# A transformer block on one core: the last expert pair's down projection as one half and two quarters of the columns, the last quarter scattered in fp32, and each token tile finished and stored by itself

## What is computed

```python
def _expert_choice_ffn(h, w_router, w_e_gate, w_e_up, w_e_down):
    cap = EC_CAPACITY * s // N_EXPERTS          # 64 tokens for each of 16 experts
    aff = softmax(h @ w_router)
    vals, idx = lax.top_k(swapaxes(aff, 1, 2), cap)
    xg = h[idx]
    a, u = xg @ w_e_gate, xg @ w_e_up           # (64, 2048) @ (2048, 1024), each expert
    y = (silu(a) * u) @ w_e_down                # (64, 1024) @ (1024, 2048)
    return zeros(s, d).at[idx].add(y * vals)

x = x + gt2 * _expert_choice_ffn(h2, ...)
return _rmsnorm(x, g_final)                     # x * rsqrt(mean(x * x) + eps) * g_final
```

## Time and profile before

| | |
|---|---|
| median of 3 runs | 2383.43 us (2383.26 to 2383.95) |
| span of the profiled execution | 2385.8 us (its own time is not listed apart from the three runs) |
| busy in the span | PE 2188.0 (92%), DVE 849.1 (36%), ACT 531.7 (22%), POOL 116.0 (5%) |
| HBM | 622.40 MB read, 12.58 MB written |
| mean granted TensorE clock | 0.977 of 2.4 GHz |
| issue to landing, e_slot<-in_w_e_down, 1 MB each | 23.5 us median |

### The profile page before, as it was taken

The page is one execution under the profiler, slowest core; times in us unless marked ns, Lnnn a source line. Parts: engine busy times, 40 slices in busy tenths (PEclk is TensorE's granted clock), DMA queues, the critical chain, the costliest instruction groups (busy, mean ns, idle before and its releaser), DMA issues.

```text
span 2385.8 us, 27009 instructions
## 1 busy us (share of the span) xinstructions
PE 2188.0 (92%) x10146; PEld 1361.5 (57%) x10146; DVE 849.1 (36%) x1107; ACT 531.7 (22%) x949; POOL 116.0 (5%) x89
## 2 busy tenths in 40 slices
PE   5989899899999998999999969999898989898985
PEld 3777677688874444588887744444444444444432
DVE  3472463866652335444533340111111111111114
ACT  3244242122223335411322221000000000000002
POOL 0000018700000001000000000000000000000000
PEclk9999999999999999999999979999999999999998
DMA  6975495688871100243432259999999999999996
GB/s 248 333 256 180 164 306 163 221 290 320 308 240 40 26 14 0 71 144 120 169 115 87 73 214 415 421 421 422 422 422 422 422 422 422 422 422 422 422 417 243
DMA packets 166844, 635.91 MB, mean 267 GB/s; under 512 B 23118, under 2 KB 35708, under 8 KB 118012
## 3 DMA queue, kind: packets, MB, share of 16 engines
q1 hardware_dynamic: 161692, 625.60, 67.7%
q10 hardware_dynamic: 4608, 8.39, 0.9%
q0 software_dynamic: 480, 1.05, 0.4%
HBM read 622.40 MB, written 12.58 MB: 266 GB/s over the span
## 4 chain that ended last, share of the span: by engine, by line
PE 71%; DMA 19%; DVE 5%; issue 2%; ACT 2%; SPq 1%; DVEq 0%; ACTq 0%
PE bank L606 20%; DMA e_slot<-in_w_e_up 13%; PE bank L608 11%; PE bank L932 9%; PE bank L943 8%; PE bank L906 5%; PE bank L775 3%; PE bank L667 3%; DMA e_slot<-in_w_e_down 2%; DMA stage<-in_w_in 1%; PE bank L822 1%; PE bank L742 1%; PE bank L765 1%; DVE ada_acc L1436 1%; PE bank L762 1%
## 5 line engine op out<-in xcount | busy, mean ns | idle before, releaser
L932 PE MATMUL bank<-e_slot,xgT 128*64 128x512 f32 x2048 | 459.1, 596 | 61.9 <-DMA e_slot<-in_w_e_up 48.7
L932 PEld LDWEIGHTS bank<-e_slot,xgT 128*64 128x64 f32 x2048 | 151.2, 137 | 346.0 <-issue 342.9
L1367 DVE TENSOR_TENSOR w_lo<-stage,w_hi 128x1024 fp32r<-128x1024 f32 (+1 forms) x168 | 214.8, 1278 | 369.8 <-ACT w_hi L1043 369.0
L1043 ACT ACTIVATE w_hi<-stage 128x1024 fp32r<-128x1024 f32 (+1 forms) x168 | 175.2, 1044 | 663.9 <-PE bank L606 371.3
L943 PE MATMUL bank<-e_slot,heT 128*64 128x512 f32 x896 | 196.9, 595 | 0.0
L1436 DVE SCALAR_TENSOR_TENSOR ada_acc<-ada_tile,siluc,ada_acc 128x1024 f32<-128x1024 f32 x120 | 168.2, 1402 | 15.2 <-DMA ada_tile<-in_w_ada 11.7
L606 PE MATMUL bank<-hT_hi,w_lo 128*128 128x512 f32 x512 | 160.6, 395 | 9.8 <-DVE w_lo L1367 9.8
L606 PE MATMUL bank<-hT_hi,w_hi 128*128 128x512 f32 x512 | 160.8, 396 | 0.0
L606 PE MATMUL bank<-hT_lo,w_hi 128*128 128x512 f32 x512 | 159.6, 393 | 0.0
L1296 ACT ACTIVATE xgT<-bank,modcol,a 128x128 f32<-128x128 f32 x128 | 48.1, 456 | 449.4 <-PE bank L906 449.4
L1782 DVE TENSOR_TENSOR x<-x,bank 128x512 f32<-128x512 f32 x128 | 79.5, 683 | 178.4 <-PE bank L917 178.3
(11 more groups left out here) (268 smaller groups left out, 2671.8 us busy)
## 6 DMA issues: line engine op xcount, KB each, us to landing
e_slot<-in_w_e_gate SPq DMA_DIRECT2D x128, 1024.0 KB, 20.4
e_slot<-in_w_e_up SPq DMA_DIRECT2D x128, 1024.0 KB, 22.8
e_slot<-in_w_e_down SPq DMA_DIRECT2D x128, 1024.0 KB, 23.5
ada_tile<-in_w_ada SPq DMA_DIRECT2D x160, 512.0 KB, 5.4
stage<-in_w_in SPq DMA_DIRECT2D x96, 512.0 KB, 6.6
sh_tile<-in_w_ada SPq DMA_DIRECT2D x32, 512.0 KB, 7.2
stage<-in_w_out SPq DMA_DIRECT2D x32, 512.0 KB, 3.6
sig_gates<-sig ACTq DMA_DIRECT2D x32, 256.0 KB, 2.5
```

Source lines behind the costliest of these rows:

```text
L932: last = mm(bank[b0 + h][64 * e:64 * e + 64, :], xgT[:, k, e, :], e_slot[(c + e) % NSLOT][:, j, h * W:(h + 1) * W], start=k == 0, stop=k = ...
L1043: A(w_hi[:, c % NSPLIT, :, 0:width], stage[:, c % NSTAGE, :, 0:width], ACT.Copy).then_inc(hi_ready, 1)
L1367: V.tensor_tensor(w_lo[:, c % NSPLIT, :, 0:width], stage[:, c % NSTAGE, :, 0:width], w_hi[:, c % NSPLIT, :, 0:width].bitcast(F32), ALU.sub ...
```

## The change

- **Chunks.** In the last pair the first four groups still hold half the columns (0 to 1023), in another assignment of rows. The last eight chunks hold one quarter of the columns and four rows for each partition, in runs of 2 KB: two groups for columns 1024 to 1535, two for 1536 to 2047 (`down_quarter_chunks`). `heT` is transposed to match (`dj` is 4 there).
- **TensorE order.** `scatter(p, 0)`, `(p, 1)` and `(p, 2)` stand after the first, second and third group of the quarters. The last quarter isn't split into y_hi and y_lo: one fp32 matmul for each tile takes `y32[3]` itself, behind the loop.
- **ScalarE.** No `y_round` for quarter 3. The Sqrt table is loaded before `final_squares(2)`, and there is a Sqrt for each tile, placed between the last squares.
- **VectorE.** Sums, reciprocals and results tile by tile; each result in two halves of 128 x 1024.
- **SP.** Eight stores of 512 KB in place of four of 1 MB.

```diff
--- before.py
+++ after.py
...
     w_down_v = w_e_down[0].rearrange("e (k p j) n -> k p e (j n)", p=P, j=DJ)
-    w_down_half_v = w_e_down[0].rearrange("e (k p j) n -> k e p j n", p=P, j=ROWS)
+    w_down_last_v = w_e_down[0].rearrange("e (k p j) n -> k e p j n", p=P, j=2 * ROWS)
...
                 stage_of, g, e = c // (2 * KG), c % (2 * KG) // 2, c % 2
                 slot = e_slot[c % NSLOT]
-                if stage_of == 2 and last_pair:
-                    half, m = g // (KG // 2), g % (KG // 2)
-                    dst, src = slot[:, :, :], w_down_half_v[m, 2 * p + e, :, :, half * 2 * W:(half + 1) * 2 * W]
+                if stage_of == 2 and last_pair and g < KG // 2:
+                    rows = slice(g % 2 * ROWS, (g % 2 + 1) * ROWS)
+                    dst, src = slot[:, :, :], w_down_last_v[g // 2, 2 * p + e, :, rows, 0:2 * W]
+                elif stage_of == 2 and last_pair:
+                    jd, u = 2 + (g - KG // 2) // 2, g % 2
+                    dst = slot[:, :, :].rearrange("p j (i n) -> p (j i) n", n=W)
+                    src = w_down_last_v[u, 2 * p + e, :, :, jd * W:(jd + 1) * W]
                 else:
                     src = (w_gate_v, w_up_v, w_down_v)[stage_of][g][:, ds(2 * p + e, 1), :]
                     dst = slot[:, :, :].rearrange("p j n -> p (j n)").unsqueeze(1)
...
             sp.wait_ge(xg_ready, 4 * PAIRS)
             sp.dma_start(gf_row[:, :], g_final.partition_broadcast(P)).then_inc(gf_in, 16)
             for t in range(T):
-                sp.wait_ge(res_ready, t + 1)
-                sp.dma_start(out_v[:, t, :], res[t][:, :]).then_inc(stored, 16)
-            sp.wait_ge(stored, 16 * T)
+                for half in range(2):
+                    sp.wait_ge(res_ready, 2 * t + half + 1)
+                    sp.dma_start(out_v[:, t, half * 2 * W:(half + 1) * 2 * W], res[t][:, half * 2 * W:(half + 1) * 2 * W])\
+                        .then_inc(stored, 16)
+            sp.wait_ge(stored, 16 * 2 * T)
         @block.tensor
...
                                       e_slot[(c + e) % NSLOT][:, 2 * j + h // 2, h % 2 * W:(h % 2 + 1) * W], start=k == 0, stop=k == 7)
                 last.then_inc(e_used, 2)
-            def down_half_chunks(p, c, half, m):
+            def down_half_chunks(p, c, m):
                 chunks_full(p, c)
                 for j in range(ROWS):
                     k = ROWS * m + j
                     for h in range(2):
                         for e in range(2):
-                            last = mm(bank[2 * half + h][64 * e:64 * e + 64, :], heT[:, k, 64 * e:64 * e + 64],
+                            last = mm(bank[h][64 * e:64 * e + 64, :], heT[:, k, 64 * e:64 * e + 64],
                                       e_slot[(c + e) % NSLOT][:, j, h * W:(h + 1) * W], start=k == 0, stop=k == 7)
+                last.then_inc(e_used, 2)
+
+            def down_quarter_chunks(p, c, jd, u):
+
+                chunks_full(p, c)
+                for i in range(2 * ROWS):
+                    k = 2 * ROWS * u + i
+                    for e in range(2):
+                        last = mm(bank[jd][64 * e:64 * e + 64, :], heT[:, k, 64 * e:64 * e + 64],
+                                  e_slot[(c + e) % NSLOT][:, i // 2, i % 2 * W:(i % 2 + 1) * W], start=k == 0, stop=k == 7)
                 last.then_inc(e_used, 2)
             def pe_pair(p, first, last_pair):
...
                     gather(4, 0)
                 for h in range(2):
                     pe.wait_ge(he_ready, 2 * p + h + 1)
-                    dj = ROWS if last_pair else DJ
+                    dj = 2 * ROWS if last_pair else DJ
                     he_rows = sg[:, h, :].rearrange("q (k p j) -> q k p j", p=P, j=dj)
                     for f in range(4):
...
                             pe.wait_ge(xg_ready, 4 * p + 3 + u)
                             gather(2 + u, u)
                 else:
-                    for half in range(2):
-                        for m in range(KG // 2):
-                            down_half_chunks(p, 4 * KG + KG * half + 2 * m, half, m)
-                            if half == 1 and ROWS * (m + 1) == 4:
-                                scatter(p, 0)
-                    scatter(p, 1)
+                    for m in range(KG // 2):
+                        down_half_chunks(p, 4 * KG + 2 * m, m)
+                    for i in range(4):
+                        down_quarter_chunks(p, 5 * KG + 2 * i, 2 + i // 2, i % 2)
+                        if i < 3:
+                            scatter(p, i)
             pe.wait_ge(sel_ready, 1)
             pe.wait_ge(xn2_ready, T)
...
             with pe.Fori(1, PAIRS - 1) as p:
                 pe_pair(p, False, False)
             pe_pair(PAIRS - 1, False, True)
-            for jd in (2, 3):
-                scatter(PAIRS - 1, jd)
+            pe.wait_ge(y32_ready, 4 * PAIRS)
+            for t in range(T):
+                pe.wait_ge(scat_added, 16 * (PAIRS - 1) + 8 + t + 1)
+                mm(bank[4 + t][:, :], selT[:, t * P:(t + 1) * P].bitcast(F32), y32[3][:, :], start=True, stop=True).then_inc(scat_done, 1)
         @block.scalar
...
                     act.wait_ge(scat_done, 16 * p + 4 * (jd - 1))
                 A(y_hi[jd % 2][:, :], y32[jd][:, :], ACT.Copy).then_inc(yhi_ready, 1)
+            def final_square(jd, t):
+                act.wait_ge(scat_added, 16 * (PAIRS - 1) + 4 * jd + t + 1)
+                act.wait_ge(sq2_seq, 16 + 4 * jd + t)
+                A(junk3[:, :], x1[:, t, jd * W:(jd + 1) * W], ACT.Square, accum_out=ssq2[:, t, jd:jd + 1]).then_inc(sq2_seq, 1)
+
             def final_squares(jd):
                 for t in range(T):
-                    act.wait_ge(scat_added, 16 * (PAIRS - 1) + 4 * jd + t + 1)
-                    act.wait_ge(sq2_seq, 16 + 4 * jd + t)
-                    A(junk3[:, :], x1[:, t, jd * W:(jd + 1) * W], ACT.Square, accum_out=ssq2[:, t, jd:jd + 1]).then_inc(sq2_seq, 1)
+                    final_square(jd, t)
+
+            def final_std(t):
+                act.wait_ge(std3_ready, t + 1)
+                A(ssq[:, 12 + t:13 + t], ssq[:, 8 + t:9 + t], ACT.Sqrt, bias=eps_c[:, :], scale=1.0 / D).then_inc(rstd3_ready, 1)
             def act_pair(p, first, last_pair):
                 if first:
...
             final_squares(0)
             y_round(PAIRS - 1, 2)
             final_squares(1)
-            y_round(PAIRS - 1, 3)
+            load_table(ACT.Sqrt)
             final_squares(2)
-            final_squares(3)
-
-
-            act.wait_ge(std3_ready, 1)
-            A(ssq[:, 12:16], ssq[:, 8:12], ACT.Sqrt, bias=eps_c[:, :], scale=1.0 / D).then_inc(std3_ready, 1)
+            for t in range(T):
+                final_square(3, t)
+                if t:
+                    final_std(t - 1)
+            final_std(T - 1)
         @block.vector
...
                 V.tensor_tensor(y_lo[jd][:, :], y32[jd][:, :], y_hi[jd % 2][:, :].bitcast(F32), ALU.subtract)\
                     .then_inc(ylo_ready, 1)
+            def add_scattered_tile(p, jd, t):
+                dve.wait_ge(scat_done, 16 * p + 4 * jd + t + 1)
+                V.tensor_tensor(x1[:, t, jd * W:(jd + 1) * W], x1[:, t, jd * W:(jd + 1) * W], bank[4 + t][:, :],
+                                ALU.add).then_inc(scat_added, 1)
+
             def add_scattered(p, jd):
                 for t in range(T):
-                    dve.wait_ge(scat_done, 16 * p + 4 * jd + t + 1)
-                    V.tensor_tensor(x1[:, t, jd * W:(jd + 1) * W], x1[:, t, jd * W:(jd + 1) * W], bank[4 + t][:, :],
-                                    ALU.add).then_inc(scat_added, 1)
+                    add_scattered_tile(p, jd, t)
             def y_added(p):
...
                     for jd in range(2):
                         y_rest(p, jd)
                     add_scattered(p, 0)
-                    for jd in (2, 3):
-                        y_scaled(p, jd, EC)
+                    y_scaled(p, 2, 5 * KG + KG // 2)
                     y_rest(p, 2)
                     add_scattered(p, 1)
-                    y_rest(p, 3)
                     add_scattered(p, 2)
-                    add_scattered(p, 3)
+                    y_scaled(p, 3, EC)
...
             dve_pair(PAIRS - 1, False, True)
-            dve.wait_ge(sq2_seq, 32)
-            V.tensor_reduce(ssq[:, 8:12], ssq2[:, :, :], AX.X, ALU.add).then_inc(std3_ready, 1)
-            dve.wait_ge(std3_ready, 2)
-            link(V.reciprocal(rstd[:, 0:4], ssq[:, 12:16]))
+            def square_sum(t):
+                dve.wait_ge(sq2_seq, 16 + 12 + t + 1)
+                V.tensor_reduce(ssq[:, 8 + t:9 + t], ssq2[:, t, :], AX.X, ALU.add).then_inc(std3_ready, 1)
+
+            def results(t):
+                dve.wait_ge(rstd3_ready, t + 1)
+                link(V.reciprocal(rstd[:, t:t + 1], ssq[:, 12 + t:13 + t]))
+                for half in range(2):
+                    cols = slice(half * 2 * W, (half + 1) * 2 * W)
```

(17 more changed lines are left out.)

## The result

| | before | after |
|---|---|---|
| median of 4 runs | 2383.48 us (2383.26 to 2383.95) | 2371.62 us (2369.59 to 2374.02) |
| ratio, 95% interval | | 0.9956 (0.9942 to 0.9970) |
| profiled execution | span 2385.8 | time 2374.02, span 2372.1 |
| busy DVE, ACT | 849.1, 531.7 us | 853.7, 531.9 us |

The kernel is 11.9 us faster. So the sign was right and the forecast gain too small. The question is whether the change did more than I had summed, or whether the sum was set against the wrong base.

A forecast was written before the change was run, and what follows sets the result against it. The experts were taken to be bound by weight loads, leaving a 30.19 us tail after the last. Cutting it to 19.72 with 1.88 lost ahead gains 8.6, off 2383.43: 2374.8 us, range 2373.1 to 2378.6.

The forecast's parts named there:

- The sum: Whole kernel: tail 10.47 us shorter, 1.88 lost ahead, gain 8.6, taken off the median 2383.43 to give 2374.8 us.
- How the numbers follow: Range and chances for the whole kernel: 2373.1 to 2378.6 us, forecast as summed 78 in 100, faster 92 in 100.
- Part 1, the loads: Last eight w_down chunks in 2 KB runs: 391 GB/s, a pair in 5.36 us instead of 5.11.
- The far bound of 335 GB/s: Quarters' loads at the rate of short bursts: 25.0 us for all eight against 20.4, or 4.6 late.
- the rival built on it: Quarters' 2 KB loads run at 335 GB/s: y_3 starts 4.6 us late instead of 1.88, time 2377.5; 7 in 100.
- Part 2, TensorE's order: Last groups with scatters between: 5.62 us apart, the last 0.9 after its weights, y_3 starts 1.88 us later.
- Part 3, the tail: From y_3's start: first result at 5.35 us, last half ends at 16.00, last store 3.72 later; 19.72 instead of 30.19.
- B: Stretch from the start of y_3, the last quarter's scaling, to the span's end; forecast 19.72 us instead of 30.19.
- The half clock: Rival at the last fp32 scatter: matmuls at 1.2 GHz, tiles 1.71 us apart, 3.4 more, 2378.2; 7 in 100.
- slip in the tile-by-tile norm: Rival in the tail: unseen waits between ScalarE and VectorE cost 0.76 us each, three give about 2377.1; 5 in 100.
- The eight stores: Rival at the end: stores on SP's queue don't overlap, kernel slower at 2386.5 to 2388.9 us; 2 in 100.
- A: Stretch from the last group before the quarters to y_3's start; the forecast put y_3 1.88 us later than before.

The follow-up runs named there:

- b_again: The kernel before, run again unchanged: median 2381.79 us over 12 runs, ratio 0.9997 to the kernel before.
- no_lo: The changed kernel without the y_lo matmuls in the last pair's scatters of quarters 0 to 2: 2372.16 us (1 run).
- runs_4k: The changed kernel with the last eight chunks loaded in 4 KB runs, bringing quarters 2 and 3 other weights than they need: 2379.51 us (1 run).
- whole_stores: The changed kernel with four stores of 1 MB, each issued when both halves of a tile are ready: 2377.47 us (1 run).
- hi_lo: The changed kernel with the last quarter's scatter in fp32r on y_hi and y_lo, like the others: 2372.48 us (1 run).
- split_scatter: The changed kernel with tiles 2 and 3 of quarter 2's scatter moved behind the last group: median 2370.37 us (12 runs), ratio 0.9949 to the kernel before.
- a_again: The changed kernel, run again unchanged: median 2370.62 us over 6 runs, ratio 0.9951 to the kernel before.
- split_scale: The changed kernel with the last scaling and fp32 scatter split into halves of columns: 2374.16 us (1 run).

## Why the prediction missed its range

**The base and its scatter were wrong, not the mechanism.** The failed step is in "The sum" and in "How the numbers follow". I took the gain off "the median of the runs, 2383.43" and allowed "some of the runs' scatter (0.7)" for its uncertainty, which is what three runs within 0.7 us of each other seemed to say. The 29 runs beside b_again show that the same program takes from 2375.4 to 2389.5 us with a median of 2381.7. With that base the forecast of 8.6 gives 2373.1 and the local gain of 9.4 gives 2372.3, against medians of after of 2371.62 and 2370.62. So of the 3.2 us between forecast and result 1.7 are the base, 0.8 the two terms below, and 0.6 are left to the scatter of four runs. The two terms alone would not have left the range: 9.4 off the base that I took is 2374.0. A sign was there to read: the profiled span of 2385.8 was longer than every listed time, although a span is shorter than its own time (by 1.9 in after: 2374.02 against 2372.1). So that execution took some 2387.7 (an estimate), 4.3 above the median, and one such run beside three close ones says that the spread is several us. I put the profiled execution 2.4 above the median and gave that no place in the range. One thing stays open: drawn at random from the 29 times, four lie within 0.7 us of each other only about once in 1000 draws (my estimate). The first four may have had something in common that the later ones had not; no run shows what.

**Part 1, the loads.** Expected: 5.36 for a pair of 2 KB chunks. Measured: 5.41 for the first, and 5.34 to 5.41 for the three behind it in no_lo, where nothing else rules. Right. The far bound of 335 GB/s, and the rival built on it, did not come.

**Part 2, TensorE's order.** Expected: groups 5.62 apart, no DMA wait at the last, y_3 after 3.70, together 1.88 lost. Measured: 5.62 three times, 3.70, 1.92. Right; runs_4k and no_lo confirm that TensorE's pace rules in it and the loads only at its start.

**Part 3, the tail.** Expected: TensorE at 0.80, first result at 5.35. Measured: 0.81, 5.34. The clock stayed at 1.00. Two terms were mis-sized:

- A tile of results was put at 2.78, 2.78 and 2.61; it took 2.66, 2.65 and 2.59. The chain of waits of after shows why:

```profile
2361.07 0.07 DVE ssq L1863
2361.13 0.08 DVE rstd L1867
2361.21 0.02 issue
2361.24 2.48 DVE res L1870 x2
```

  The sum and the reciprocal have records of 0.15 each but add 0.07 and 0.08 to the path, where nothing is waited for. I had charged a wait's 0.21 and a full 0.17. The last result ended at 15.72, not 16.00.
- From there to the end I put 3.72; it was 3.14, since the stores no longer queue. I had named this and kept it for the range. whole_stores splits it.

Together B is 18.86 instead of 19.72, and the local gain 9.4 instead of 8.6.

**The rivals.** The half clock was rightly thought unlikely for this order, with 0.86 us of idle time ahead of the scatter; hi_lo shows it at 2.24. A wait for weights can bring it too: the quarter behind a wait of 1.75 took 3.65 as the others, but in split_scatter the group behind a wait of 2.15 took 5.35. The Trainium skill (TensorE: Matmul & The Clock Gate, "HAM oscillation — how this bites in real kernels") tells of a kernel whose groups of matmuls start at the low clock behind waits for DMA of some 3 to 5 us; here, once, a shorter one did it. No slip in the tile-by-tile norm came. The eight stores overlapped: issued over 9.42 us, each landed after 2.7, and halves beat whole ones by 1.20. The Trainium skill's advice to batch to 1 MiB or more (DMA: Bandwidth & Descriptors, "Measured (HBM→SBUF, 128 partitions, SWDGE, issued from GpSimd)") is given there for the share of peak bandwidth, by loads; for the stores on which the end waits, the smaller ones were faster here.

## What to carry to other kernels

Work that follows the last load should be cut so that as little as possible hangs on the last piece: moving two quarters' scatter ahead of the last group gained 8.2 us together with the plain fp32 scatter, and cost 1.9 together with the shorter runs of the loads, because TensorE, which had 1.5 us of slack a group, got 2.0 us of extra work. Finish tile by tile, and halve what is stored last. And before a median is used as a base, ask how far runs of the same program lie apart: where a profiled span lies outside the listed times, the range needs several us for that alone, and local stretches between two fixed instructions tell an edit of 0.1 us where single times don't tell one of 5.

## What was not expected of the hardware

- A program on one core, unchanged, spread over 14 us (0.6%). In the first fifth a load stood on the chain for 16 to 21 us in eight profiles and not at all in five, with TensorE's granted clock at 340 to 380 us 0.87 in b_again and 1.00 in a_again; but two profiles of one program drew apart by 3.0 to 3.9 us more between 658 us and the start of A.
- TensorE's clock was half behind 2.24 us of idle time (hi_lo) and behind a DMA wait of 2.15 (split_scatter), and stayed at full behind 0.86 and 1.75 (after). The length of the last idle stretch doesn't decide alone: in split_scale the clock was 0.60 from 2314.5 to 2318 us, behind idle stretches of 1.32, 0.87 and 0.73, where after has the same rows (1.32, 0.87, 0.73) and kept it.
- Loads of 1 MB in runs of 2 KB came at a pair in 5.34 to 5.41 us beside a full queue, against 5.12 for runs of 4 KB: 5%, not the 18% of the stretch with short bursts.
